# Reordering the ends of the expert items in a YOCO trunk kernel, with down weights loaded two rows per partition

## The reference

```python
# attention of layer 0, per block of 128 queries
mask = k_chunk[None, :] <= q_chunk[:, None]          # chunks of 64 frames
p = softmax(where(mask, s, -inf))
...
# mixture of layer 1
probs = softmax(xt @ router); top_p, top_i = top_k(probs, 2)
gates = one_hot(top_i) weighted by top_p / sum(top_p)
for e in range(8):
    y = y + gates[:, e:e+1] * ((silu(xt @ Wg[e]) * (xt @ Wu[e])) @ Wd[e])   # Wg, Wu 1024x2816, Wd 2816x1024
```

## Time and profile before

| | |
|---|---|
| runs, median of three | 1222.37 us |
| profiled execution, device time | 1218.11 us |
| its span, first to last instruction | 1216.0 us |
| TensorE busy | 1105.5 us, 91% |
| VectorE, ScalarE busy | 622.3 us, 528.0 us |
| weight loads | 341.9 MB on the queue q1 |
| mean granted TensorE clock | 0.967 of full speed |

### The profile page before, as it was taken

How to read it: one execution, slowest core, us unless ns; L and a number is a source line. 1 busy time by engine, 2 the same in 40 slices (tenths; PEclk the granted TensorE clock), 3 DMA queues, 4 the chain that set the end, 5 groups by cost and what they waited for, 6 DMA issues and landing times.

```text
span 1216.0 us, 16289 instructions
## 1 busy us (share of the span) xinstructions
PE 1105.5 (91%) x5724; PEld 811.0 (67%) x5724; DVE 622.3 (51%) x688; ACT 528.0 (43%) x578; POOL 19.1 (2%) x94
## 2 busy tenths in 40 slices
PE   7999999999999978999968989988989989999774
PEld 6867888888898767775436776436777777643231
DVE  6745555455563468773026874007786987300001
ACT  6444544344436537652026663015665666201001
POOL 1100000000000000000000000000000000000000
PEclk9889999999999979999989999998999999999999
DMA  9933456555454218888999987999987988899995
GB/s 353 307 103 104 163 185 200 178 176 208 142 191 147 85 60 310 323 307 284 402 410 405 367 333 263 391 409 409 397 329 268 355 312 310 283 402 409 409 402 212
DMA packets 122458, 343.51 MB, mean 282 GB/s; under 512 B 12893, under 2 KB 39562, under 8 KB 122378
## 3 DMA queue, kind: packets, MB, share of 16 engines
q1 hardware_dynamic: 122234, 341.94, 76.7%
q10 hardware_dynamic: 144, 0.52, 0.1%
HBM read 341.37 MB, written 1.05 MB: 282 GB/s over the span
## 4 chain that ended last, share of the span: by engine, by line
PE 68%; SPq 11%; issue 6%; DMA 5%; DVE 5%; ACT 4%; POOL 0%; DVEq 0%; POOLq 0%; ACTq 0%
PE ps L1452 18%; PE ps L1453 18%; PE ps L1454 17%; PE ps L1457 13%; SPq L360 6%; SPq L364 5%; ACT whi L546 4%; DMA raw<-moe_w_down_dram 3%; DMA raw<-moe_w_gate_up_dram 3%; DVE wlo L951 1%; DVE hlo L1220 1%; DVE xlo L1176 1%; PE ps L1784 1%; PE ps L1467 1%; DVE h L1133 1%
## 5 line engine op out<-in xcount | busy, mean ns | idle before, releaser
L546 ACT ACTIVATE whi<-raw 128x2048 fp32r<-128x2048 f32 (+1 forms) x195 | 335.5, 1724 | 298.4 <-PE ps L1454 257.4
L951 DVE TENSOR_TENSOR wlo<-raw,whi 128x2048 fp32r<-128x2048 f32 x151 | 346.3, 2297 | 217.8 <-ACT whi L546 216.5
L1452 PE MATMUL ps<-whi,xhi 128*128 128x512 f32 (+3 forms) x688 | 270.1, 393 | 11.8 <-DVE gu L1214 4.0
L1453 PE MATMUL ps<-whi,xlo 128*128 128x512 f32 (+3 forms) x688 | 265.7, 386 | 0.0
L1454 PE MATMUL ps<-wlo,xhi 128*128 128x512 f32 (+3 forms) x688 | 264.8, 385 | 0.0
L1457 PE MATMUL ps<-raw,xs 128*64 128x512 f32 (+2 forms) x1024 | 158.7, 462 | 11.0 <-DMA raw<-moe_w_gate_up_dram 10.8
L1452 PEld LDWEIGHTS ps<-whi,xhi 128*128 128x128 f32 x688 | 133.5, 194 | 40.4 <-issue 8.9
L1454 PEld LDWEIGHTS ps<-wlo,xhi 128*128 128x128 f32 x688 | 133.5, 194 | 25.1
L1453 PEld LDWEIGHTS ps<-whi,xlo 128*128 128x128 f32 x688 | 133.5, 194 | 23.2
L1457 PEld LDWEIGHTS ps<-raw,xs 128*64 128x64 f32 x1024 | 67.0, 137 | 97.8 <-issue 64.2
L1452 PE MATMUL ps<-whi,hhi 128*128 128x512 f32 x264 | 106.2, 402 | 0.0
(11 more groups left out here) (282 smaller groups left out, 979.6 us busy)
## 6 DMA issues: line engine op xcount, KB each, us to landing
raw<-moe_w_gate_up_dram SPq DMA_DIRECT2D x256, 512.0 KB, 5.6
raw<-moe_w_down_dram SPq DMA_DIRECT2D x176, 512.0 KB, 11.1
raw<-moe_w_gate_up_dram SPq DMA_DIRECT2D x96, 384.0 KB, 8.7
raw<-ffn_w_gate_up_dram SPq DMA_DIRECT2D x44, 512.0 KB, 4.9
raw<-ffn_w_down_dram SPq DMA_DIRECT2D x22, 512.0 KB, 4.1
raw<-kv_shared_w_dram SPq DMA_DIRECT2D x16, 512.0 KB, 4.1
raw<-moe_w_gate_up_dram SPq DMA_DIRECT2D x32, 256.0 KB, 9.0
raw<-mla_w_o_dram SPq DMA_DIRECT2D x8, 512.0 KB, 14.5
```

What stands on the lines that cost most here:

```text
L546: return nc.scalar.activation(o, i, ACT.Copy, scale=scale)
L951: V.tensor_tensor(wlo[:, s, :].rearrange("p a w -> p (a w)"), raw[:, (hh // 2) % RAW, :], whi[:, s, :].bitcast(F32).rearrange("p a w -> p ...
L1452: pe.matmul(o, a_hi, b_hi, start=start, stop=False, skip_group_check=True)
L1453: pe.matmul(o, a_lo, b_hi, start=False, stop=False, skip_group_check=True)
```

## The change

- **Transposes.** The groups' transposes stand on TensorE after units 9, 11, 17, 19, 23 and 25, and `high` and `low` one unit later (`HIDDEN_AT`).
- **Selection.** The transposes of `sel` leave `begin` and stand after the down unit d == 8, in big and small items. ScalarE's `transposed` moves up with them.
- **Small item's end.** The scatter comes ahead of `begin` instead of behind it. `gathered_high` and `gathered_low` come ahead of the next item's splits. VectorE instead of ScalarE copies `ys`, and adds in (`add_in`) between the third and fourth split.
- **Down weights.** A down unit is one transfer of 1 MB in which partition p gets rows 2p and 2p+1, 8 KB in a piece, instead of two transfers with 4 KB rows. The last down unit stays as it was. So that features meet their rows, the transposes of `gm` read every second column (`interleaved`).
- **Pairs.** The hardware loop over the two pairs is written out.
- **Chunk mask.** It is added by two fp32r products of 128 columns with the identity instead of two float32 products of one row and 64 columns.

```diff
+HIDDEN_AT = (10, 12, 18, 20, 24, 26)
...
+def interleaved(t, j):
+    w = t.shape[1]
+    if j == SUB - 1:
+        return [t[:, b * P:(b + 1) * P] for b in range(w // P)]
+    v = t.rearrange("p (u q n) -> p u n q", n=2, q=P)
+    return [v[:, b // 2, b % 2, :] for b in range(w // P)]
...
+                elif x < FU - 1:
+                    of = w_dn[(x - GU) * 256:(x - GU + 1) * 256, :].rearrange("(p n) d -> p (n d)", n=2)
+                    sp_eng.dma_start(raw[:, u % RAW, :], of).then_inc(landed[u % RAW], 16)
...
-            with sp_eng.Fori(0, PAIRS) as p:
+            for p in range(PAIRS):
...
# ScalarE, small item
-                    for x in range(2):
-                        split_high_unit(H_MOE + 2 * x, p + 1, g + 1)
                     gathered_high(p + 1, g + 1)
-                    split_high_unit(H_MOE + 2 * 2, p + 1, g + 1)
...
-                act.wait_ge(small_used, p * FU + FU)
-                copy(ys[:, :], ps[:, 4, :]).then_inc(ys_ready, 1)
...
# VectorE, small item
                 if following == "big":
-                    for x in range(2):
-                        split_low_unit(H_MOE + 2 * x, p + 1)
                     gathered_low(p + 1)
-                    for x in range(2, 5):
+                dve.wait_ge(small_used, p * FU + FU)
+                V.tensor_copy(ys[:, :], ps[:, 4, :]).then_inc(ys_ready, 1)
+                if following == "big":
+                    for x in range(3):
                         split_low_unit(H_MOE + 2 * x, p + 1)
                 add_in(g)
+                if following == "big":
+                    for x in range(3, 5):
+                        split_low_unit(H_MOE + 2 * x, p + 1)
...
# TensorE, big item
-                    for b in range(w // P):
-                        last = pe.transpose(ps[:, TR_BANK, b * P:(b + 1) * P], gm[:, j % 2, b * P:(b + 1) * P], ident[:, :])
+                    for b, block in enumerate(interleaved(gm[:, j % 2, 0:w], j)):
+                        last = pe.transpose(ps[:, TR_BANK, b * P:(b + 1) * P], block, ident[:, :])
...
-                    if x in (9, 10, 17, 18):
-                        transposes({9: 0, 10: 1, 17: 2, 18: 3}[x])
+                    if x + 1 in HIDDEN_AT:
+                        transposes(HIDDEN_AT.index(x + 1))
...
+                    if d == 8:
+                        selection(following, next_i)
...
# TensorE, small item
-                if following is not None:
-                    begin(following, next_i, g + 1)
                     pe.wait_ge(selN_ready, g + 2)
...
+                if following is not None:
+                    begin(following, next_i, g + 1)
...
# chunk mask
-                for a in (CHUNK, 128 + 192):
-                    last = mm(ps[:, b, a:a + CHUNK], half_mask[0:1, 0:P], half_mask[0:1, P:P + CHUNK], False, True)
+                for a in (0, SEQ):
+                    last = mm(ps[:, b, a:a + P], ident_r[:, :], half_mask_r[:, :], False, True)
```

More of the change, by code:

```diff
@@ L99, in transfers @@
 def transfers(x):
-    return len(segments(x)) if x < GU else 2
+    return len(segments(x)) if x < GU else 1 if x < FU - 1 else 2
+def interleaved(t, j):
[4 more added lines that the diff above has]
+    return [v[:, b // 2, b % 2, :] for b in range(w // P)]
 def small_place(f):
@@ L184, in build @@
         diag, = over(("diag", [P, TC, P], F32))
[L186 removed]
+        _, ang, ang_k, cos, sin, invf, posi, posf, mx, nmx, rs, rr, css, cfac, qscale, half_mask, half_mask_r = over(
             ("gap2", [P, 6 * 1024 + 1280 + 2560], F32), ("ang", [P, TC, 32], F32), ("ang_k", [P, TC, 32], F32),
@@ L488, in _ @@
                                     base=0, pattern=[[1, P]], channel_multiplier=-1)
+            nc.gpsimd.affine_select(out=half_mask[:, CHUNK:P], in_=half_mask[:, CHUNK:P], compare_op=ALU.is_ge, fill=NEG,
+                                    base=-CHUNK, pattern=[[0, CHUNK]], channel_multiplier=1)
             nc.gpsimd.affine_select(out=neg_from[:, :], in_=neg_ones[:, :], compare_op=ALU.is_ge, fill=0.0,
@@ L767, in big @@
                         silu({7: 0, 15: 2, 21: 4}[x])
-                    if x in (10, 11, 18, 19, 24, 25):
-                        high({10: 0, 11: 1, 18: 2, 19: 3, 24: 4, 25: 5}[x])
+                    if x in HIDDEN_AT:
+                        high(HIDDEN_AT.index(x))
+                    if x == FU - 2:
+                        transposed(g + 1)
                     if x == FU - 1:
@@ L821, in small @@
                 if following == "big":
-                    for x in range(3, 5):
+                    for x in range(5):
                         split_high_unit(H_MOE + 2 * x, p + 1, g + 1)
@@ L900, in _ @@
                 split_high_unit(H_MOE + 2 * x)
-            with act.Fori(0, PAIRS) as p:
+            for p in range(PAIRS):
                 big(p, 2 * p, "small")
@@ L1225, in big @@
                         gate({7: 0, 15: 2, 21: 4}[x])
-                    if x in (10, 11, 18, 19, 24, 25):
-                        low({10: 0, 11: 1, 18: 2, 19: 3, 24: 4, 25: 5}[x])
+                    if x in HIDDEN_AT:
+                        low(HIDDEN_AT.index(x))
                     if x == 14:
@@ L1425, in _ @@
                 split_low_unit(H_MOE + 2 * x)
-            with dve.Fori(0, PAIRS) as p:
+            for p in range(PAIRS):
                 big(p, 2 * p, 2 * p, "small", 2 * p + 1)
@@ L1759, in small_unit, with selection @@
                 last.then_inc(small_used, 1)
-            def begin(following, i, g):
+            def selection(following, i):
                 if following == "big":
@@ L1802, in big @@
                     last.then_inc(used, 2)
-                    if d in (1, 2):
-                        transposes(d + 3)
+                    if GU + d + 1 in HIDDEN_AT:
+                        transposes(HIDDEN_AT.index(GU + d + 1))
                     if d == 5:
@@ L1824, in transposes @@
                         pe.wait_ge(hT_ready, p * SMALL_GROUPS + j)
-                    for b in range(SMALL_WIDTH[j] // P):
-                        last = pe.transpose(ps[:, TR_BANK, b * P:(b + 1) * P], gm[:, j % 2, b * P:(b + 1) * P], ident[:, :])
+                    for b, block in enumerate(interleaved(gm[:, j % 2, 0:SMALL_WIDTH[j]], SUB - SMALL_GROUPS + j)):
+                        last = pe.transpose(ps[:, TR_BANK, b * P:(b + 1) * P], block, ident[:, :])
                     last.then_inc(small_tr, 1)
@@ L1852, in small @@
                         gather(g + 1)
+                    if d == 8 and following is not None:
+                        selection(following, next_i)
                 if following is not None:
-                    begin(following, next_i, g + 1)
                     pe.wait_ge(selN_ready, g + 2)
@@ L1950, in _ @@
             gather(0)
+            selection("big", 0)
             begin("big", 0, 0)
-            with pe.Fori(0, PAIRS) as p:
+            for p in range(PAIRS):
                 big(p, 2 * p, "small", p)
```

13 lines of the change are left out of this document (6 added, 7 removed).

## The result

Four executions of the changed kernel took 1169.02 to 1173.77 us, median 1170.36, against 1221.82 for four of the kernel before. The ratio is 0.9592, with a 95% interval of 0.9551 to 0.9633: faster by 4.1%. The profiled execution took 1170.41 us, 47.7 less than the profiled 1218.11; the sum had said 44.5 less.

The account below looks back on a forecast made before the run. Small items were taken as bound by loads, big ones by TensorE. Terms -1.8 - 23.3 - 8.5 - 17.3 + 8.5 - 2.1 = -44.5 us took 1218.1 to 1173.6, plus 0.35% 1178 us; range 1160 to 1202.

Parts of the forecast that it names:

- What bounds the kernel: Whole kernel: small items bound by loads, big ones by TensorE, whose savings return while load pauses are left to fill.
- Transposes two units apart: Groups' transposes in big items: twelve TensorE waits for `hlo` disappear with about 0.6 us to spare, -23.3 us.
- The clock behind these waits: Half-clock stretches of 3.4 us after the `hlo` waits: five of six go, -8.5 us, bounds 0 and -10.2.
- From a small item to a big one: Two such places: unit 3 starts 14.4 us after ScalarE's first split instead of 24.2 and 21.9, -17.3 us.
- The selection within big items: Earlier selection waits 1.0 us in three big items, 3.8 in the third, perhaps a 1.7 us dip: +8.5 us.
- Down weights in one transfer: Load-bound down units of small items: 8 KB rows save 0.05 us each over 40 units, -2.1 us, bounds 0 and -4.
- The rival of slow 8 KB rows: Down unit loads: 4.3 us a unit, 72 us more, 1250 us and more; chance 4%.
- Strided transposes: Weight loads of `gm` reading every second float: cost taken as 0, upper bound +11.2 us for 80 doubled loads.
- a sign that it is wrong: Transposes' weight loads longer than 140 ns, or down units landing further apart than 2.56 us, would make the prediction wrong.
- Chunk mask: Eight attention heads, TensorE-bound: mask products take about 0.42 us instead of 0.65, -1.8 us.
- The 0.35%: Whole kernel: median of the runs, 1222.4 us, over the profiled 1218.1, added to turn 1173.6 into 1178 us.

Follow-up runs that it names:

- relief of some 30 us: Changed kernel with one of three products left out in units 2 to 32 of the second big item: 1166.13 us; in the fourth instead: 1157.66 us.
- two transfers: Changed kernel with down units loaded as two transfers with 4 KB rows and plain transposes again: 1168.91 us, ratio 0.9625 to the kernel before.

## Why the prediction was right

Forecast 1178 us, measured 1170; the profiled execution was to lose 44.5 us and lost 47.7. The steps one by one:

- **What bounds the kernel.** That big items are TensorE's, small ones the loads', and that pauses turn TensorE's gains into time, was right. In the second big item 16.4 us were to be taken out of 18.2 of pause. By bytes, which compare the same work, 21.5 us of pause were there and 2.9 are left, so 18.6 were taken; it all fitted, with little to spare. A relief of some 30 us in that item is worth 3 us, and in the fourth, where pause was left, 8 to 12. The difference is the rule at work.
- **Transposes two units apart, -23.3 us.** The waits went; undone, they came back as 23.0 us. The margin was 0.76 us against 0.6.
- **The clock behind these waits, -8.5 us.** Five of six half-speed stretches were booked as gone. All six are gone, 1.7 us more; undone, five return, at 509, 690, 871, 987 and 1008 us, only in part behind the same transposes as before. The mechanism was right, and which waits the clock follows was not foretold. The waits together with the clock are worth 31 to 35 us in the runs and 32.6 between the profiles, against 31.8 booked.
- **From a small item to a big one, -17.3 us.** Unit 3 was put at 14.4 us and stands at 14.3 and 14.4. Undoing the order alone costs 14 to 18 us, undoing the loop alone 4: the two together can't be told from the 17.3, or are a little more. The loop put back costs 4.91 us of idle time and a slow clock instead of 2.05.
- **The selection within big items, +8.5 us.** Waits of 0.92, 0.92, 3.74 and 0.90 us against 1.0, 1.0, 3.8 and 1.0. The clock is at half for 3.4 or 6.8 us at the long wait in nine of the ten profiles that have it (6.8 in that of the changed kernel, 3.4 in its second) and not at all in one (two transfers): 1.7 to 3.4 us lost where 1.7 was booked. Undone, the kernel is 7 to 10 us faster. This is the part that ought to be taken back.
- **Down weights in one transfer, -2.1 us.** 2.49 us a unit against 2.50; 3.0 us for 40 units. The forecast's division came out a little low (2.63 less 2.55 is 0.08 us for 10.7 packets, 7.3 ns each), and it left out 20 units of big items that have become bound by loads, so that the term is some 4 us, at the end of its bounds. The rival of slow 8 KB rows is out: loads run at 406 to 410 GB/s. Rows were not cut: the profile counts 110,934 - 100,618 = 10,316 packets of 8 KB or more, where before there were 80. The Trainium skill, "DMA: Bandwidth & Descriptors", section "SWDGE vs HWDGE vs iDMA", has packets at most 4096 B preferably, in its table on the descriptors that GpSimd builds. For these loads, which SyncE issues, the trace shows no such limit, and the longer ones are the better.
- **Strided transposes, 0.** Right in the time, for the reason given, and wrong in what was expected of the rows: weight loads were to stay at 140 ns and take 207. The prediction had named longer loads as a sign that it is wrong; the sign came, and the cost did not. The loads are hidden beside the products, except for 11 ns each. The Trainium skill, "SBUF — State Buffer", section "Door 1: The DMA port swizzle", has two accesses to one 16-byte line at full bandwidth; for a weight load of every second float the trace disagrees: 207 ns against 139 is neither free nor doubled but half-way.
- **Chunk mask, -1.8 us.** The products shortened as priced (0.65 to 0.44). The step that failed is that nothing else would change there. The clock's dip lasted longer, 10.2 to 13.7 us instead of 6.8, and at that place nothing was gained. The old mask in the changed kernel ran 3.5 us longer all the same, from causes that stay open, so the runs neither confirm nor refute the term of 1.8 as a whole.

The sum fell short by 3.2 us. The sixth half-speed stretch (1.7) and the 8 KB rows (3 to 4 for 2.1) go that way, the clock at the third big item's end (up to 1.7 more than booked) goes the other. The runs know single terms to a few microseconds only, so the 3.2 us aren't settled, and that the sum came this near owes something to errors that cancel. The 0.35% between the profiled time and the median, added for the forecast, did not appear in the runs after (1170.41 profiled, 1170.36 median), and made the other 4 us.

## What to carry to other kernels

When two engines take turns at the bound, count the pauses of the loads first. They say how much of a gain on the other engine can arrive: the same 30 us or so spared on TensorE brought 3 us in one item and 8 to 12 us in another. A chain of three engines between two uses of one bank is hidden by distance in the program, as long as the distance exceeds the chain by some tenths of a microsecond. Moving a step earlier helps where its operand is already there and costs where it is not: the same move of the selection left no wait in small items, where it was one part of a better order, and cost 7 to 10 us in big ones.

## What the runs showed of the hardware that was not expected

- A hardware loop's new beginning left TensorE idle 2.05 us in the kernel before, and 4.91 us in the changed kernel with the loop put back, for a cause not shown; ScalarE loads its function tables (1.28 us) again for the body.
- TensorE's weight load of every second float takes 207 ns, of consecutive ones 139. The product beside it grows by 11 ns only (283 against 272).
- 8 KB rows land 1 MB in 2.49 us, 4 KB rows in 2.565: a gain of 3%.
- Shorter products at the start of an attention did not shorten it, since TensorE's granted clock stayed at half for 10.2 to 13.7 us in ten profiles, and for 6.8 us in the two with the longer products.
- Twelve waits of 1.9 to 2.0 us were followed by a half-speed stretch of 3.4 us six times before and five times when they were put back, at partly other waits; one wait of 3.74 us, the same in ten profiles, went with 0, 3.4 or 6.8 us.
